# When VectorE makes the low half of a weight split in the attentions, and when it takes the difference of the two maps

## The chip, the cores and the metric

The kernel runs on one core of a Trainium2 chip. The metric is the device time of one execution in microseconds (us), the median of three runs. TensorE (PE) does the matrix products and the transposes, ScalarE (ACT) the activations, VectorE (DVE) the elementwise work and the row reductions, GpSimd (POOL) the small reciprocal square roots, and SyncE (SP) issues the loads of the weights.

## The reference, cut to what matters

Four transformer layers over 256 tokens of width 1024, batch 1, float32. The first two (`first_block`) have a sparse attention and a gated unit; the next two (`second_block`) are these:

```python
def second_block(x, c, ...):
    cond = silu(c)
    for layer in range(2):
        sh1, sc1, g1, sh2, sc2, g2 = split(cond @ ada_w[layer] + ada_b[layer], 6)
        h = modulate(rms_norm(x, norm_mix[layer]), sh1, sc1)
        y = even_mixer(h, ...) if layer % 2 == 0 else odd_mixer(h, ...)
        x = x + g1 * y
        h = modulate(rms_norm(x, norm_mlp[layer]), sh2, sc2)
        x = x + g2 * squared_relu_mlp(h, mlp_w1[layer], mlp_w2[layer])
```

The even mixer has a latent attention with 8 heads (called the MLA attention below) and a dilated attention. The odd mixer has a differential attention and a block attention (MoBA). In the differential attention each head has two maps, and their difference meets the values:

```python
sc = einsum('bqhmd,bkhmd->bmhqk', q, k) * scale      # m: two maps
p = softmax(where(causal, sc, NEG_INF))
pd = p[:, 0] - lam * p[:, 1]
o = einsum('bhqk,bkhe->bqhe', pd, v)
```

## The kernel before, in words

**Products.** Every product is made of three single-pass products: weights and activations are split into a high half and a low half (high x high, high x low, low x high, lines 1422 to 1424). The activations are stationary (XTH/XTL or HTH/HTL, 128 x 128), the weights move, 512 (or 384) columns at a time, and the sum stays in a PSUM bank. The 256 tokens are two tiles t = 0, 1.

**Weight split.** The weights come as items of up to 4 x 512 columns. SP loads an item into a buffer of `RAW` (9 buffers, which share their memory with `WB`). `split` then has two parts: ScalarE copies the raw item into another buffer as the high half (printed L1545, the line of ScalarE's helper), and VectorE subtracts it from the raw item, in place, which gives the low half (L1745). VectorE's part waits for ScalarE's (`wh`), and TensorE's product waits for VectorE's (`wl`). Up to three items are split ahead of their use.

**Order.** Nothing schedules at run time. The program first writes one list, `order`, with calls `do(part, ...)`; then each engine's program walks through the list and emits its own instructions of each part. So each engine does its work strictly in the order of the list. `advance()` puts the splits of the next items into the list, ahead of the products (`slot`) of the current one.

**Attention.** `attention(units, ...)` works on units (some heads of one tile of 128 queries), in steps k. In a step it lists:

1. `scores(k)`: TensorE's products into PSUM, and `soft(k)`: VectorE's row maximum (L1938) and its negative (L1948), then ScalarE's exponentials with row sums into `E`;
2. `turns(k-1)`: TensorE's transposes of the unit before (L1447), after two or three filling products (`busy`, L1407), and a copy of them into `PET`, by ScalarE or VectorE (L1818) in turn;
3. the filler: some steps of a generator with other work, here the products of later input projections, with their splits, their copies to `H`, and the norm and rotation of queries and keys. One such rotation (`qk_rope`, called a rotation below) is five operations of VectorE: L2086, L1861, L1862, L1864, L1865. A sum of squares (`qk_sq`, L2081) follows ScalarE's square, and POOL's reciprocal root comes between the two;
4. `ends(k)` for a unit with `diff`: `differ`, VectorE's difference of the two maps in `E` (L1957, L1960, L1964 twice, L1968 twice), for which the transposes of the next step wait; and `ends(k-1)` for a unit with `joint` (one small sum, L1952);
5. `values(k-2)`: TensorE's products with the values (L1532).

The three attentions with units that concern this case are the MLA attention (6 units), the dilated one (8 units, `joint`) and the differential one (4 units, `diff`). Units 0 and 1 of the differential attention have 128 keys, units 2 and 3 have 256. Its filler makes two input projections (4 items), four rotations and, after step 3, the transposes of the rotated queries and keys of MoBA (`turn_qk`, L1447 <- H). When a tile's values are complete, `diff_out` copies them to `MIX`, squares them into `SCR` (ScalarE) and sums them up (VectorE, L2113); a rotation uses `SCR` too, and the square waits for the rotation listed before it.

## Time and profile before

| | |
|---|---|
| Median of 3 runs | 1432.17 us (1431.86 to 1433.95) |
| The profiled execution's own time | 1432.39 us |
| Its span, first to last instruction | 1430.6 us |
| PE busy | 1343.2 us (94%) |
| DVE busy | 942.3 us (66%) |
| ACT busy | 657.7 us (46%) |
| POOL busy | 109.4 us (8%) |
| Mean granted TensorE clock | 0.984 of full speed |

All times in the text are us from the start of the span. Busy times are shares of that one execution. "Idle before <- releaser" behind an instruction is how long its engine stood still before it, and which instruction let it go on. A start is exact, while the duration of an instruction overlaps the next one's on ScalarE and VectorE, so the distance from start to start is what counts in a sum.

### The profile page before, as it was taken

How to read it: one execution, taken by the hardware profiler on the slowest of the kernel's cores; microseconds unless marked ns; L12 is line 12 of the kernel's file. 1: busy time of each engine (PE TensorE's matmuls, PEld its weight loads, DVE VectorE, ACT ScalarE, POOL GpSimd, SP SyncE). 2: the span in 40 equal slices, each digit the busy share in tenths (PEclk: the TensorE clock that was granted, in tenths of full speed). 3: DMA queues.
4: the chain of work that ended last, by engine and by line, in shares of the span. 5: the costliest groups of instructions: out<-in, count | busy, mean ns of one | idle time of the engine just before them, and what ended most of it. 6: DMA issues, size and time to landing. Idle time of an engine off the chain costs nothing.

```text
span 1430.6 us, 16545 instructions
## 1 busy us (share of the span) xinstructions
PE 1343.2 (94%) x6684; PEld 1108.5 (77%) x6684; DVE 942.3 (66%) x1249; ACT 657.7 (46%) x886; POOL 109.4 (8%) x156
## 2 busy tenths in 40 slices
PE   6999999999989999999798898999998978999998
PEld 6767888887967788888698876888886857788886
DVE  4857777766675777775657856766666776554444
ACT  4544533333463543333365454454545544454542
POOL 1010000000020000000114300000003320000000
PEclk9999999999999999999998999999999999999999
DMA  9505577773612667775153204666663430355550
GB/s 366 194 1 206 219 307 295 293 270 124 272 60 93 229 246 294 294 294 200 61 195 107 100 30 148 264 263 266 262 267 139 156 118 1 118 206 186 188 186 30
DMA packets 40236, 269.87 MB, mean 189 GB/s; under 512 B 4544, under 2 KB 4560, under 8 KB 11872
## 3 DMA queue, kind: packets, MB, share of 16 engines
q1 hardware_dynamic: 37712, 259.31, 48.6%
q0 software_dynamic: 2304, 8.46, 1.6%
q8 instruction: 53, 0.87, 0.2%
q10 hardware_dynamic: 144, 1.05, 0.2%
q14 instruction: 23, 0.19, 0.0%
HBM read 267.75 MB, written 1.05 MB: 188 GB/s over the span
## 4 chain that ended last, share of the span: by engine, by line
PE 81%; DVE 10%; ACT 4%; issue 2%; POOL 1%; DMA 1%; SPq 0%; POOLq 0%; ACTq 0%; DVEq 0%
PE ps L1422 23%; PE ps L1424 23%; PE ps L1423 23%; PE ps L1447 5%; PE ps L1532 2%; PE ps L1508 1%; ACT WB L1545 1%; DVE WB L1745 1%; PE ps L1435 1%; PE ps L1407 1%; DMA RAW<-W 1%; DVE st L2008 1%; DVE X L2018 1%; ACT E L1545 1%; DVE st L1938 1%
## 5 line engine op out<-in xcount | busy, mean ns | idle before, releaser
L1745 DVE TENSOR_TENSOR WB<-RAW,WB 128x2048 fp32r<-128x2048 f32 (+4 forms) x210 | 453.3, 2162 | 285.0 <-ACT WB L1545 284.9
L1545 ACT ACTIVATE WB<-RAW 128x2048 fp32r<-128x2048 f32 (+4 forms) x210 | 379.7, 1810 | 233.0 <-PE ps L1424 220.2
L1422 PE MATMUL ps<-WB,XTH 128*128 128x512 f32 (+3 forms) x1176 | 459.6, 391 | 19.9 <-DVE XTL L1750 12.9
L1424 PE MATMUL ps<-WB,XTL 128*128 128x512 f32 (+3 forms) x1176 | 449.5, 382 | 0.0
L1423 PE MATMUL ps<-WB,XTH 128*128 128x512 f32 (+3 forms) x1176 | 449.1, 382 | 0.0
L1422 PEld LDWEIGHTS ps<-WB,XTH 128*128 128x128 f32 x1176 | 224.4, 191 | 60.8 <-DVE XTL L1750 13.2
L1424 PEld LDWEIGHTS ps<-WB,XTL 128*128 128x128 f32 x1176 | 224.0, 190 | 38.6
L1423 PEld LDWEIGHTS ps<-WB,XTH 128*128 128x128 f32 x1176 | 224.7, 191 | 35.0
L1422 PE MATMUL ps<-WB,HTH 128*128 128x512 f32 (+1 forms) x452 | 178.5, 395 | 2.5 <-DVE HTL L1826 1.9
L1424 PE MATMUL ps<-WB,HTL 128*128 128x512 f32 (+1 forms) x452 | 177.8, 393 | 0.0
L1423 PE MATMUL ps<-WB,HTH 128*128 128x512 f32 (+1 forms) x452 | 177.7, 393 | 0.0
L1804 DVE SCALAR_TENSOR_TENSOR ACC<-RAW,colv,ACC 128x512 f32<-128x512 f32 x168 | 126.2, 751 | 5.1
L1545 ACT ACTIVATE HTH<-ps 128x512 fp32r<-128x512 f32 (+1 forms) x58 | 32.1, 585 | 159.6 <-PE ps L1447 159.4
L1422 PEld LDWEIGHTS ps<-WB,HTH 128*128 128x128 f32 x452 | 85.2, 188 | 22.1 <-DVE HTL L1826 2.4
L1344 POOL TENSOR_SCALAR st<-st 128x1 f32<-128x1 f32 (+3 forms) x42 | 24.3, 578 | 1004.6 <-DVE st L2011 538.3
L1424 PEld LDWEIGHTS ps<-WB,HTL 128*128 128x128 f32 x452 | 85.2, 188 | 19.5
L1423 PEld LDWEIGHTS ps<-WB,HTH 128*128 128x128 f32 x452 | 85.3, 189 | 19.1
L1545 ACT ACTIVATE GB<-ps 128x512 f32<-128x512 f32 (+1 forms) x94 | 46.4, 499 | 93.4 <-PE ps L1424 93.3
L1545 ACT ACTIVATE E<-ps,st 128x128 f32<-128x128 f32 (+1 forms) x104 | 42.4, 420 | 74.5 <-DVE st L1948 74.5
L1826 DVE TENSOR_TENSOR HTL<-ps,HTH 128x512 fp32r<-128x512 f32 x54 | 35.8, 687 | 39.9 <-ACT HTH L1545 39.9
L1407 PE MATMUL ps<-cstb 128*128 128x512 bf16 x228 | 61.6, 386 | 0.0
L1346 POOL TENSOR_TENSOR st<-st,cst 128x1 f32<-128x1 f32 (+3 forms) x42 | 46.5, 1107 | 3.5
(177 smaller groups left out, 1045.0 us busy)
## 6 DMA issues: line engine op xcount, KB each, us to landing
RAW<-W SPq DMA_DIRECT2D x220, 1024.0 KB, 4.9
RAW<-W SPq DMA_DIRECT2D x14, 768.0 KB, 4.3
RAW<-W SPq DMA_DIRECT2D x12, 728.0 KB, 5.7
VEC<-vecd POOLq DMA_DIRECT2D x10, 512.0 KB, 7.1
RAW<-W SPq DMA_DIRECT2D x8, 512.0 KB, 3.3
RAW<-W SPq DMA_DIRECT2D x4, 576.0 KB, 3.8
GB<-xTd ACTq DMA_DIRECT2D x1, 1024.0 KB, 7.9
X<-xd SPq DMA_DIRECT2D x1, 1024.0 KB, 15.9
```

The costliest lines, as they stand in the source:

```text
L1344: eng.tensor_scalar(x, x, scale, eps, ALU.mult, ALU.add).then_inc(*own.up())
L1346: eng.tensor_tensor(x, x, MH.to_broadcast([128, x.shape[1]]), ALU.pow).then_inc(*up("rsqrt", key))
L1407: eng.matmul(banks[b][:, :], identb, cstb[:, 0:512], start=True, stop=True)
L1422: eng.matmul(ps, xh, hi[:, j, c0:c0 + cw], start=first and j == 0, stop=False)
L1423: eng.matmul(ps, xh, lo[:, j, c0:c0 + cw], start=False, stop=False)
L1424: op = eng.matmul(ps, xl, hi[:, j, c0:c0 + cw], start=False, stop=last and j == n - 1)
L1447: op = eng.transpose(banks[b][0:rows, j * 128:j * 128 + 128], src, ident)
L1532: op = eng.matmul(banks[b][:, c0:c0 + dv], PET[:, u["i"], blk * 128:blk * 128 + 128], val, start=(j == 0), stop=(j == len(lst) - 1))
L1545: return eng.activation(dst, src, f, **k)
L1745: eng.tensor_tensor(WB[:, it["raw"], 0:w], RAW[:, it["raw"], 0:w], WB[:, it["high"], 0:w].bitcast(F32), ALU.subtract).then_inc(*up("wl", n))
L1804: op = eng.scalar_tensor_tensor(out=ACC[:, a, :], in0=view[:, j, :], scalar=cond[:, kt:kt + 1], in1=ACC[:, a, :], op0=ALU.mult, op1=ALU.add)
L1826: eng.tensor_tensor(HTL[:, r2:r2 + 2, :], banks[b][:, :].rearrange("p (n q) -> p n q", n=2), HTH[:, r2:r2 + 2, :].bitcast(F32), ALU.subtra ...
```

## The change

`split` becomes two parts with names of their own: `high` (ScalarE) and `low` (VectorE). Outside of attentions both stand side by side in the list as before. Inside `attention` (`cur["lag"]`) the item goes on a list `low`, and its low half is listed later: at the next `advance()`, ahead of its own product, or right behind the `scores`/`soft` of the next step, whichever comes first. And `ends` of a unit with `diff` stands ahead of the filler, directly behind `turns`. `mid_at` is a new argument that nothing sets.

```diff
+        def lows(its=None):
+            for it in list(low) if its is None else [it for it in its if it in low]:
+                low.remove(it)
+                do("low", it)
+
         def advance(most=NBUF):
             loads()
+            lows()
...
-                    do("split", it, after)
+                    do("high", it, after)
+                    low.append(it)
+                    if not cur["lag"]:
+                        lows()
...
             def slot(it, t):
                 b, fr = ps[t]
+                lows([it])
...
+            cur["lag"] = True
             for k in range(n + 2):
                 if k < n:
                     if "bank" not in units[k]["ok"]:
                         units[k]["ok"]["bank"] = take()
                     scores(units[k], 0 if k else first)
+                lows()
                 if 1 <= k <= n:
                     turns(units[k - 1], pads[k - 1] if k <= len(pads) else 2)
+                if k < n and units[k]["diff"]:
+                    ends(units[k])
                 if filler is not None:
                     for _ in range(steps if isinstance(steps, int) else steps[k]):
                         next(filler, None)
-                if k < n and units[k]["diff"]:
-                    ends(units[k])
                 if 1 <= k <= n and units[k - 1]["joint"]:
                     ends(units[k - 1])
                 if k >= 2:
                     values(units[k - 2])
+            cur["lag"] = False
+            lows()
```

No instruction is added or taken away, and TensorE, ScalarE, POOL and SP keep their order, instruction by instruction. Only VectorE's order moves, at three places. The changed kernel's line numbers are 19 higher here (L1745 becomes L1764, L2081 becomes L2100, L1938 becomes L1957).

**Place 1, VectorE, MLA attention, around the row maximum of unit 3** (the fourth low half, 128x1536). Before:

```order
L2081 TENSOR_REDUCE st<-TB 128x6
L1745 TENSOR_TENSOR WB<-RAW,WB 128x1536
L1938 TENSOR_REDUCE st<-ps 128x2
L1948 TENSOR_SCALAR st<-st 128x2
L2086 TENSOR_TENSOR H<-H,st 128x384
L1861 TENSOR_TENSOR SCR<-H,TB 128x384
```

Changed:

```order
L2100 TENSOR_REDUCE st<-TB 128x6
L1957 TENSOR_REDUCE st<-ps 128x2
L1967 TENSOR_SCALAR st<-st 128x2
L1764 TENSOR_TENSOR WB<-RAW,WB 128x1536
L2105 TENSOR_TENSOR H<-H,st 128x384
L1880 TENSOR_TENSOR SCR<-H,TB 128x384
```

The low half went from ahead of the row maximum to behind it. The same holds for the second and third low half (units 1 and 2); the first stands behind two sums of squares and not ahead of them. In the dilated attention one low half and one small sum changed places.

**Place 2, VectorE, differential attention, unit 2** (with its row maximum, its difference, and the rotation of the filler). Before:

```order
L1948 TENSOR_SCALAR st<-st 128x4
L1745 TENSOR_TENSOR WB<-RAW,WB 128x2048
L2086 TENSOR_TENSOR H<-H,st 128x512
L1861 TENSOR_TENSOR SCR<-H,TB 128x512
L1862 TENSOR_TENSOR SCR<-H,TB 128x512
L1864 TENSOR_TENSOR H<-SCR 128x8x32
L1865 TENSOR_TENSOR H<-SCR 128x8x32
L2081 TENSOR_REDUCE st<-GB 128x8
L1957 RECIPROCAL st<-st 128x4
L1960 TENSOR_SCALAR st<-st,lam 128x2
L1964 TENSOR_SCALAR E<-E,st 128x256 x2
L1968 SCALAR_TENSOR_TENSOR E<-E,st 128x256 x2
```

Changed:

```order
L1967 TENSOR_SCALAR st<-st 128x4
L1976 RECIPROCAL st<-st 128x4
L1979 TENSOR_SCALAR st<-st,lam 128x2
L1983 TENSOR_SCALAR E<-E,st 128x256 x2
L1987 SCALAR_TENSOR_TENSOR E<-E,st 128x256 x2
L2105 TENSOR_TENSOR H<-H,st 128x512
L1880 TENSOR_TENSOR SCR<-H,TB 128x512
L1881 TENSOR_TENSOR SCR<-H,TB 128x512
L1883 TENSOR_TENSOR H<-SCR 128x8x32
L1884 TENSOR_TENSOR H<-SCR 128x8x32
L2100 TENSOR_REDUCE st<-GB 128x8
```

The difference of unit 2 went ahead of the rotation and the sum, and the low half went behind the row maximum of unit 3, so it stands between that and the difference of unit 3. Units 0, 1 and 3 move alike; the low half of step 1 stands between unit 1's row maximum and the copy to `PET` that precedes its difference.

**Place 3, VectorE, differential attention, step 4** (the copy of unit 3's transposes and the last rotation). Before:

```order
L2113 TENSOR_REDUCE st<-SCR 128x4
L1818 COPY PET<-ps 128x512
L2086 TENSOR_TENSOR H<-H,st 128x512
L1861 TENSOR_TENSOR SCR<-H,TB 128x512
L1862 TENSOR_TENSOR SCR<-H,TB 128x512
```

Changed:

```order
L2132 TENSOR_REDUCE st<-SCR 128x4
L1764 TENSOR_TENSOR WB<-RAW,WB 128x2048
L1837 COPY PET<-ps 128x512
L2105 TENSOR_TENSOR H<-H,st 128x512
L1880 TENSOR_TENSOR SCR<-H,TB 128x512
L1881 TENSOR_TENSOR SCR<-H,TB 128x512
```

The fourth low half of this attention, which stood behind the row maximum of unit 3, now stands ahead of the copy and the last rotation.

## Rows read from the trace of the kernel before

**Rows 1.** The page's part 4: the chain that ended last, by engine

```profile
PE 81%; DVE 10%; ACT 4%; issue 2%; POOL 1%; DMA 1%; SPq 0%; POOLq 0%; ACTq 0%; DVEq 0%
```

**Rows 2.** Waits of PE, 1137 to 1190: total us, times, longest

```profile
PE ps L1447 <- DVE E L1968: 12.0, 3, 5.4
```

**Rows 3.** Timeline of PE, differential attention: start, us, instruction [idle before <- releaser]

```profile
1156.00 0.44 PE L1447 MATMUL ps<-cst,E 128*128 128x128 f32 x2 [3.63 <-DVE E L1968]
...
1169.00 0.66 PE L1447 MATMUL ps<-cst,E 128*128 128x128 f32 x4 [3.01 <-DVE E L1968]
...
1181.63 1.11 PE L1447 MATMUL ps<-cst,E 128*128 128x128 f32 x4 [5.40 <-DVE E L1968]
...
1185.95 1.88 PE L1447 MATMUL ps<-cst,H 128*128 128x128 f32 x8
1187.65 1.07 PE L1532 MATMUL ps<-H,PET 128*128 128x128 f32 x8
```

**Rows 4.** Timeline of DVE, same stretch

```profile
1150.70 0.42 DVE L1818 COPY PET<-ps 128x256 f32<-128x256 f32 x1
...
1155.86 1.28 DVE L1938 TENSOR_REDUCE st<-ps 128x2 f32<-128x512 f32 x2
...
1161.42 2.29 DVE L1745 TENSOR_TENSOR WB<-RAW,WB 128x2048 fp32r<-128x2048 f32 x1 [4.07 <-ACT WB L1545]
1163.62 0.68 DVE L2086 TENSOR_TENSOR H<-H,st 128x512 f32<-128x512 f32 x1
...
1166.95 0.17 DVE L1957 RECIPROCAL st<-st 128x4 f32<-128x4 f32 x1
...
1168.86 1.28 DVE L1938 TENSOR_REDUCE st<-ps 128x2 f32<-128x512 f32 x2
...
1176.84 0.68 DVE L2086 TENSOR_TENSOR H<-H,st 128x512 f32<-128x512 f32 x1
...
1179.57 0.17 DVE L1957 RECIPROCAL st<-st 128x4 f32<-128x4 f32 x1
...
1181.49 0.68 DVE L2113 TENSOR_REDUCE st<-SCR 128x4 f32<-128x512 f32 x1
1182.78 0.69 DVE L1818 COPY PET<-ps 128x512 f32<-128x512 f32 x1 [0.61 <-PE ps L1447]
1183.39 0.68 DVE L2086 TENSOR_TENSOR H<-H,st 128x512 f32<-128x512 f32 x1
```

**Rows 5.** Timeline of ACT, same stretch

```profile
1157.38 0.47 ACT L1545 ACTIVATE E<-ps,st 128x256 f32<-128x256 f32 x1 [4.54 <-DVE st L1948]
...
1159.19 0.39 ACT L1545 ACTIVATE PET<-ps 128x256 f32<-128x256 f32 x1
...
1179.75 0.63 ACT L1545 ACTIVATE SCR<-MIX 128x512 f32<-128x512 f32 x1 [3.49 <-DVE H L1865]
...
1188.76 0.60 ACT L1545 ACTIVATE MIX<-ps 128x512 f32<-128x512 f32 x1 [0.29 <-PE ps L1532]
```

**Rows 6.** Timeline of DVE, MLA attention

```profile
794.92 0.69 DVE L1938 TENSOR_REDUCE st<-ps 128x2 f32<-128x512 f32 x1
...
799.17 1.76 DVE L1745 TENSOR_TENSOR WB<-RAW,WB 128x1536 fp32r<-128x1536 f32 x1 [0.71 <-ACT WB L1545]
801.84 0.69 DVE L1938 TENSOR_REDUCE st<-ps 128x2 f32<-128x512 f32 x1 [0.91 <-PE ps L1514]
...
808.78 0.68 DVE L1938 TENSOR_REDUCE st<-ps 128x2 f32<-128x512 f32 x1
```

**Rows 7.** Timeline of PE, MLA attention

```profile
810.77 0.66 PE L1447 MATMUL ps<-cst,E 128*128 128x128 f32 x4 [3.06 <-ACT E L1545]
```

**Rows 8.** Stretches: us, busy (count) of PE, PEld, DVE, ACT, POOL; granted clock, DMA share, GB/s

```profile
802.60:816.40 13.80, 10.74 (x60) 9.63 (x59) 13.42 (x33) 4.18 (x14) 6.31 (x8) 0.88 0.01 4
...
812.00:815.70 3.70, 3.70 (x14) 3.70 (x13) 3.63 (x10) 0.00 (x0) 2.12 (x3) 0.54 0.00 0
...
1181.60:1187.80 6.20, 6.17 (x30) 6.17 (x31) 4.60 (x8) 1.19 (x2) 1.20 (x2) 0.51 0.00 0
```

More of the change, by code:

```diff
@@ L290, in program @@
         cur = {"chunk": 0, "item": 0, "load": 0, "ahead": 0, "pairs": 3, "acc": 0, "sum": 0, "id": 0, "col": 0, "turn": 0, "buf": 0,
-               "ada": None}
+               "ada": None, "lag": False}
         bufs = [(n, []) for n in range(NBUF)]
+        low = []
         acc_free = [[], []]
@@ L417, in linear, with linear2 @@
             yield
-        def linear2(name, lhs, after, evacs, mid, pad=(0, 0)):
+        def linear2(name, lhs, after, evacs, mid, pad=(0, 0), mid_at=0):
             ia, ib = chunk_items(name), chunk_items(name)
@@ L428, in slot @@
                 its = (ia, ib)[c]
+                lows([it])
                 do("mm", it, t, lhs, [(b, 0, it["w"], (gs[c], t) if it is its[-1] else None)], it is its[0],
@@ L441, in linear2 @@
                             advance(1)
-                    elif it is ia[0]:
+                    elif it is ia[mid_at]:
                         mid()
@@ L471, in one @@
                 end = last and n == len(its) - 1
+                lows([it])
                 do("mm", it, t, lhs, [(ps[t][c][0], c * 512, 512, (g, t, c) if end else None) for c in range(2)],
@@ L1547, in scalar_program, with high @@
             eng.dma_start(GBT, xTd.rearrange("p (k n) -> p k n", k=8)).then_inc(*landed("xT", 0))
-            def split(it, after):
+            def high(it, after):
                 n, w = it["id"], it["n"] * it["w"]
@@ L1728, in diff_out @@
                 act(SCR[:, 0:512], MIX[:, t, 0:512], ACT.Square).then_inc(*up("diff_sq", t))
-            parts = dict(split=split, x0=x0, setup=setup, turn=turn, halves=halves, ffn_turn=ffn_turn,
+            parts = dict(high=high, x0=x0, setup=setup, turn=turn, halves=halves, ffn_turn=ffn_turn,
                          modulate=modulate, hin=hin, lat=lat, gelu=gelu, sel_score=sel_score, sgu_ln=sgu_ln,
@@ L1740, in vector_program, with low @@
             own = Own(events, "dve_own")
-            def split(it, _):
+            def low(it):
                 n, w = it["id"], it["n"] * it["w"]
@@ L2123, in diff_norm @@
                                   ).then_inc(*up("diff_norm", t))
-            parts = dict(split=split, x0=x0, setup=setup, ada=ada, sum=total, turn=turn, halves=halves,
+            parts = dict(low=low, x0=x0, setup=setup, ada=ada, sum=total, turn=turn, halves=halves,
                          ffn_turn=ffn_turn, mod_scale=mod_scale, modulate=modulate, rope_in=rope_in,
```

## The prediction

> **What bounds the kernel now.** I read the chain that ended last first: 81% of it is TensorE, 10% VectorE, 4% ScalarE [rows 1]. So a change of VectorE's order can only pay, or cost, where TensorE stands still for it. The order of the instructions says where to look: nothing moves but VectorE's, in the MLA attention, in the differential one, and by one small swap in the dilated one.
>
> The waits of TensorE in the differential attention have one entry that matters: the transposes wait three times for VectorE's difference, 12.0 us in all [rows 2]. The timeline of TensorE shows them apart: 3.63, 3.01 and 5.40 us [rows 3]. The timeline of VectorE shows why [rows 4]. A low half that stands behind the row maximum waits 4.07 us for ScalarE's high half, because ScalarE does the exponentials first, and the rotation and the difference queue behind it. In the MLA attention TensorE has one such stop, 3.06 us ahead of unit 4's transposes, for ScalarE's exponentials [rows 7], which follow unit 4's row maximum at 808.78 [rows 6]. From 802.6 to 816.4 VectorE is busy for 13.42 of 13.80 us [rows 8]: there it is the bound, without a gap.
>
> **The differential attention.** Durations are taken from start to start, which is what an in-order engine can repeat [rows 4]:
>
> - low half, 128x2048: 1161.42 to 1163.62, 2.20 us;
> - rotation and one sum of squares: 1163.62 to 1166.95, 3.33 us; rotation alone: 1176.84 to 1179.57, 2.73 us;
> - difference of a unit with 256 keys: 1166.95 to 1168.86, 1.91 us;
> - copy to `PET`: 1182.78 to 1183.39, 0.61 us;
> - from a row maximum at 1155.86 to ScalarE's first exponential at 1157.38, 1.52 us, and 1.81 us from there to the copy behind the last one [rows 4, 5]. The next instruction of VectorE can start about 1.4 us after the maximum.
>
> Now the new list, from the copy at 1150.70, until which TensorE has waited for nothing. One low half goes in ahead of it and nothing goes out before unit 2's maximum, so that maximum starts at 1155.86 + 2.20 = 1158.06. (Unit 1's difference still comes earlier: the 3.3 us of rotation and sum go behind it, against 2.20 us of low half. This shortens the first stop from 3.63 to about 2.5 us.) The exponentials of unit 2 end at 1158.06 + 1.52 + 1.81 = 1161.4. The difference follows directly: 1163.3. TensorE wants unit 2's transposes about then, so the second stop goes. Rotation and sum: 1166.6. Unit 3's maximum starts there, 2.2 us earlier than 1168.86. Then 1.4 for it and 2.20 for the low half: 1170.2 (the exponentials end at 1166.6 + 3.3 = 1169.9), and the difference ends at 1172.1. TensorE takes unit 3's transposes at 1172.2 and not at 1181.63.
>
> That is 9.4 us earlier, but it is not what is won, because **the last rotation is late next**. TensorE's following block, the eight transposes of the rotated keys that started at 1185.95 [rows 3], needs it. VectorE: rotation 2.73 (1174.8), ScalarE's square, which waits for that rotation's use of `SCR` and takes 0.63 [rows 5] (1175.5), its sum 0.68 (1176.2), the low half that now stands ahead of the copy 2.20 (1178.4), the copy 0.61 (1179.0), and the rotation until TensorE's release, 1185.95 - 1183.39 = 2.56. The sum is 1181.6, against 1185.95: **4.3 us won**. TensorE stands still ahead of it: its blocks from 1181.63 to 1185.95 took 4.32 us at half rate and about 2.2 us at full rate, so they are done by 1174.4, and an idle of 7.2 us follows.
>
> **What the clock takes back.** From 1181.6 to 1187.8 the granted clock was 0.51 of full speed [rows 8], that is 1.2 of 2.4 GHz, behind an idle of 5.40 us. The transposes at 1185.95 ran in it already; unit 3's values at 1187.65 took 1.07 us until the copy to `MIX` at 1188.76 [rows 3, 5], which is nearly full rate. After 7.2 us of idle I expect the same clock behind it, and for longer: the values would take about 1.0 us more, and the scores of MoBA's first unit, on which the next maximum waits, some tenths. I take 1.3 us, between 0 (the clock as before) and 2.1 (values and scores both at half rate). Won in this attention: 3.0 us, between 2.2 and 5.1 (the last if the transposes, too, ran at the full rate, 0.85 less).
>
> The Trainium skill, "TensorE: Matmul & The Clock Gate", section "HAM oscillation — how this bites in real kernels", says that idle gaps beyond a certain length send the clock to half, each one anew. The trace bears it out for the stops of 3.63 and 5.40 us but not for the 3.01 us one, behind which the clock stayed full. By the rule one long gap costs one slow stretch, as the single one of 5.40 us did, and the 3.0 us stand.
>
> **The MLA attention.** Four low halves of 128x1536 move, 1.76 us each [rows 6]. Count them between the row maxima. Between those of units 1 and 2 the third goes out and the second comes in; between 2 and 3 the fourth goes out and the third comes in: the same work, so the maxima at 794.92 and 801.84 stay [rows 6]. Between those of units 3 and 4 nothing goes out and the fourth comes in, where VectorE has no gap [rows 8]. The 0.71 us and 0.91 us that VectorE waited around the fourth low half [rows 6] can't pay for it, since the maximum at 801.84 waits for TensorE's scores. Unit 4's maximum goes from 808.78 to 810.5, and TensorE's stop from 3.06 to 4.8 us: **1.7 us lost**. Bounds: nothing, if some gap absorbs it, and 3.4 if the longer stop also brings a second slow stretch like that from 812.0 to 815.7, where a clock of 0.54 over 3.70 us [rows 8] cost about 1.7.
>
> **The rest, at nothing.** In the dilated attention the low half waits for ScalarE, and the small sum slips in ahead of it. The products need each low half late: the first one that moves in the differential attention is used by the block behind 1156.00, the last two by the output projection behind 1188.76. No DMA, buffer or bank changes its order.
>
> **Sum.** -3.0 + 1.7 = -1.3 us. On the profiled execution's 1432.39 us this is 1431.1, on the median, 0.2 us lower, 1430.9.
>
> **The rivals.**
>
> 1. *The forecast*: a small gain in one attention, most of it paid in the other; -1.3 us. Chance 0.50.
> 2. *Only the gain.* The MLA low half is absorbed or mostly so (by POOL or ScalarE setting the pace there and not VectorE), and the clock comes back early: -4.3 us, 1427.9. For it: the clock behind a stop isn't tied to its length alone [rows 3, 8]. Against it: 13.42 of 13.80 us busy. Chance 0.20.
> 3. *All three stops go*: -12.0 us and +1.7, 1421.9. That needs the last rotation in time, 7 us before VectorE can have it. Chance 0.03.
> 4. *No effect*: the clock takes back all that VectorE gives; within 0.5 us of 1432.2. Chance 0.17.
> 5. *Slower, by the clock.* The merged idle of 7.2 us leaves TensorE at half rate well into MoBA, where it is on the chain: one more stretch like that from 1181.6 to 1187.8, 6.20 us at 0.51 [rows 8], costs 3.0 us, on top of the upper bound of 2.1 above. With the second slow stretch in the MLA attention: -4.3 + 2.1 + 3.0 + 3.4 = +4.2, 1436.4. It decides if the rate is still half at unit 2 of MoBA. For it: the rate stayed half for 6.2 us behind 5.40 us of idle. Against it: by 1187.8 it was back, with no denser work than is there now. Chance 0.10. By the same page of the Trainium skill such stretches come again with each gap, which is this case.
>
> **How the numbers follow.** A measurement of this kernel tells about 0.2%, 2.9 us, from no change. Faster by more: rival 3, most of 2, and a slice of the forecast's lower edge: 0.25. Slower by more: most of 5, 0.09. Within: 0.66. The forecast's own range is 1429.3 to 1432.7 (3.0 and 1.7 with half of their bounds). The range for 8 in 10 takes in rival 4 and most of rival 2: 1427.9 to 1433.6, where the upper end is the worst of both terms, -2.2 + 3.4 = +1.2, with some tenths for the spread of runs.
>
> **What would show it.** In the changed kernel's profile: the wait of TensorE's transposes for `E` in the differential attention falls from 12.0 us to 3 to 5 us; a new stop of 6 to 8 us stands ahead of the eight transposes from `H`, released by the last rotation; the low halves there wait for ScalarE hardly at all; the stop at unit 4 of the MLA attention grows from 3.06 to 4.8 us. The forecast is wrong if that stop doesn't grow, if the rotation's end isn't the release, or if the clock is half well beyond the MoBA scores.

## The result, and the profile after

| | before | changed |
|---|---|---|
| Median, 11 runs each | 1433.04 us (1430.98 to 1434.43) | 1429.39 us (1427.68 to 1430.98) |
| The profiled execution | 1432.39 us | 1430.49 us |
| Its span | 1430.6 us | 1428.7 us |

The ratio of the two is 0.9978, between 0.997 and 0.9985: 3.2 us faster, between 2.1 and 4.3 (the medians themselves lie 3.65 us apart). That is just past the 0.2% that the prediction set as the bound of "no change", and the interval holds the bound. The forecast was 1.3 us faster.

The changed kernel's page, head and parts 1 and 4 (before: [rows 1] for the chain):

```profile
span 1428.7 us, 16545 instructions
...
PE 1342.2 (94%) x6684; PEld 1105.1 (77%) x6684; DVE 941.8 (66%) x1249; ACT 657.2 (46%) x886; POOL 109.8 (8%) x156
...
PE 81%; DVE 11%; ACT 3%; issue 2%; POOL 1%; DMA 1%; SPq 0%; POOLq 0%; ACTq 0%; DVEq 0%
```

The page shows next to nothing: same counts, same shares. The change is in a few stops, and these stand in the waits of PE, stretch 1137 to 1190 of the changed kernel (total us, times, longest):

```profile
PE ps L1466 <- DVE H L1884: 6.7, 2, 6.4
PE ps L1466 <- DVE E L1987: 4.4, 3, 2.5
```

The 12.0 us for the difference [rows 2] became 4.4, and a new wait of 6.7 us for the rotation took most of its place. The timeline of PE, changed kernel, shows them one by one (line numbers here are 19 higher: L1466 are transposes, L1551 values, L1527 scores, L1426 filling products):

```profile
1155.85 0.44 PE L1466 MATMUL ps<-cst,E 128*128 128x128 f32 x2 [2.51 <-DVE E L1987]
...
1164.58 0.66 PE L1466 MATMUL ps<-cst,E 128*128 128x128 f32 x4 [0.33 <-DVE E L1987]
...
1173.41 0.66 PE L1466 MATMUL ps<-cst,E 128*128 128x128 f32 x4 [1.60 <-DVE E L1987]
...
1176.13 0.66 PE L1466 MATMUL ps<-cst,H 128*128 128x128 f32 x4 [0.30 <-DVE H L1884]
...
1183.18 1.09 PE L1466 MATMUL ps<-cst,H 128*128 128x128 f32 x4 [6.40 <-DVE H L1884]
1184.06 1.91 PE L1551 MATMUL ps<-H,PET 128*128 128x128 f32 x8
```

The stops of 3.63, 3.01 and 5.40 us [rows 3] are now 2.51, 0.33 and 1.60, and one of 6.40 us stands ahead of the last four transposes of rotated keys. The timeline of DVE, changed kernel, says what each waits for:

```profile
1159.04 1.28 DVE L1957 TENSOR_REDUCE st<-ps 128x2 f32<-128x512 f32 x2
...
1162.51 0.18 DVE L1976 RECIPROCAL st<-st 128x4 f32<-128x4 f32 x1 [2.00 <-ACT E L1564]
...
1167.76 1.28 DVE L1957 TENSOR_REDUCE st<-ps 128x2 f32<-128x512 f32 x2
1169.07 0.17 DVE L1967 TENSOR_SCALAR st<-st 128x4 f32<-128x4 f32 x1
1169.15 2.28 DVE L1764 TENSOR_TENSOR WB<-RAW,WB 128x2048 fp32r<-128x2048 f32 x1
1171.35 0.17 DVE L1976 RECIPROCAL st<-st 128x4 f32<-128x4 f32 x1
...
1176.83 0.69 DVE L2132 TENSOR_REDUCE st<-SCR 128x4 f32<-128x512 f32 x1 [0.76 <-ACT SCR L1564]
1177.43 2.28 DVE L1764 TENSOR_TENSOR WB<-RAW,WB 128x2048 fp32r<-128x2048 f32 x1
1179.63 0.68 DVE L1837 COPY PET<-ps 128x512 f32<-128x512 f32 x1
1180.23 0.68 DVE L2105 TENSOR_TENSOR H<-H,st 128x512 f32<-128x512 f32 x1
...
1182.62 0.42 DVE L1884 TENSOR_TENSOR H<-SCR 128x256 f32<-128x256 f32 x1
...
1188.76 0.76 DVE L1957 TENSOR_REDUCE st<-ps 128x2 f32<-128x256 f32 x2 [0.77 <-PE ps L1533]
```

The low half at 1169.15 fills the time in which ScalarE makes the exponentials; before, the low half waited there 4.07 us [rows 4], because its high half stood behind them. The one at 1177.43 is different: it stands ahead of the copy and the last rotation, and TensorE waits all through it.

In the MLA attention, the timeline of PE, changed kernel:

```profile
813.35 1.11 PE L1466 MATMUL ps<-cst,E 128*128 128x128 f32 x4 [4.73 <-ACT E L1564]
```

3.06 us [rows 7] became 4.73.

**Where the time went, by stretches.** In one execution the time ahead of the MLA attention, where nothing moved, differs by up to 3.8 us between the kernels of this study, so spans don't compare. The distance between fixed points of the program does. The points are the first scores of the MLA, dilated and differential attentions on TensorE, MoBA's first row maximum on VectorE (1188.76 above, 1190.65 in the kernel before), and the end:

| us | MLA to dilated | dilated to differential | differential to MoBA's maximum | to the end | sum |
|---|---|---|---|---|---|
| before | 54.35 | 307.57 | 53.66 | 239.93 | 655.51 |
| changed | 56.09 | 305.96 | 50.80 | 239.93 | 652.78 |
| difference | +1.74 | -1.61 | -2.86 | 0.00 | -2.7 |

The second column holds what was not foreseen: 1.61 us won in a stretch in which the change moves no more than one low half past one small sum. TensorE's timeline of the two kernels shows where. These are the transposes for the first layer's feed-forward norm, second tile; first the kernel before:

```profile
886.51 1.27 PE L1447 MATMUL ps<-cst,MIX 128*128 128x128 f32 x8 [2.33 <-DVE MIX L2026]
```

then the changed one:

```profile
889.06 1.09 PE L1466 MATMUL ps<-cst,MIX 128*128 128x128 f32 x8 [2.33 <-DVE MIX L2045]
```

The stop is the same to a hundredth. What follows isn't. The stretches behind it (us, busy (count) of PE, PEld, DVE, ACT, POOL; granted clock, DMA share, GB/s), before:

```profile
887.50:890.90 3.40, 3.40 (x11) 2.68 (x10) 3.33 (x8) 2.21 (x6) 0.00 (x0) 0.53 0.25 43
```

and changed, with the stretches behind its two long stops:

```profile
813.60:817.00 3.40, 3.40 (x14) 3.40 (x14) 3.33 (x8) 0.52 (x2) 1.35 (x2) 0.57 0.00 0
...
890.10:893.50 3.40, 3.40 (x17) 2.77 (x16) 3.33 (x8) 2.21 (x6) 0.00 (x0) 1.00 0.21 51
...
1183.20:1189.00 5.80, 5.80 (x29) 4.12 (x31) 1.36 (x3) 1.83 (x3) 0.84 (x2) 0.54 0.00 0
```

Behind 886.5 the clock was at half (1.2 GHz), behind 889.1 at full (2.4 GHz): 11 products against 17 in 3.40 us. At half rate 3.4 us hold the work of about 1.7 us at full rate, and that is, within 0.1 us, the 1.61 us given back.

### The profile page after: what moved, and what is told of

It reads as the page before. It is cut to its first block, busy times and chain, and to the rows that moved or that the text cites. A ratio compares the mean times of both kernels' runs of the same rounds, so it can differ in the third digit from the quotient of the medians.

```text
span 1428.7 us, 16545 instructions
## 1 busy us (share of the span) xinstructions
PE 1342.2 (94%) x6684; PEld 1105.1 (77%) x6684; DVE 941.8 (66%) x1249; ACT 657.2 (46%) x886; POOL 109.8 (8%) x156
## 4 chain that ended last, share of the span: by engine, by line
PE 81%; DVE 11%; ACT 3%; issue 2%; POOL 1%; DMA 1%; SPq 0%; POOLq 0%; ACTq 0%; DVEq 0%
PE ps L1441 23%; PE ps L1443 23%; PE ps L1442 23%; PE ps L1466 4%; PE ps L1551 2%; DVE WB L1764 2%; PE ps L1527 1%; PE ps L1454 1%; PE ps L1426 1%; ACT WB L1564 1%; DMA RAW<-W 1%; DVE st L2027 1%; DVE X L2037 1%; DVE st L1957 1%; DVE X L2040 1%
## 5 line engine op out<-in xcount | busy, mean ns | idle before, releaser
L1764 DVE TENSOR_TENSOR WB<-RAW,WB 128x2048 fp32r<-128x2048 f32 (+4 forms) x210 | 453.2, 2161 | 267.4 <-ACT WB L1564 267.3
L1426 PE MATMUL ps<-cstb 128*128 128x512 bf16 x228 | 63.9, 398 | 0.0
```

The source lines that it names most:

```text
L1426: eng.matmul(banks[b][:, :], identb, cstb[:, 0:512], start=True, stop=True)
L1764: eng.tensor_tensor(WB[:, it["raw"], 0:w], RAW[:, it["raw"], 0:w], WB[:, it["high"], 0:w].bitcast(F32), ALU.subtract).then_inc(*up("wl", n))
```

## The experiments

Two questions: which part earns the gain, and does the MLA attention pay (the forecast's theory: it pays 1.7 us net) or is it paid back (the rival: the clock behind the stop at 886.5 depends on where that stop falls). The sum of stretches, as in the table above, stands beside each median. It agrees within 0.6 us, fourth_late and combo (0.9 us) apart, which says that the one execution shown is a typical one. The edits are shown shortened: `...` stands for what is left out, and a remark behind `#` stands for the argument in the call of `attention`.

| run | MLA to dilated | to differential | to MoBA's maximum | to the end | sum against before | time against before, by the ratio |
|---|---|---|---|---|---|---|
| changed | 56.09 | 305.96 | 50.80 | 239.93 | -2.7 | -3.2 |
| mla_lag_only | 56.08 | 306.07 | 53.60 | 239.93 | +0.2 | +0.3 |
| no_lag_mla | 54.37 | 307.48 | 50.83 | 240.01 | -2.8 | -3.3 |
| lag_only | 56.10 | 305.93 | 50.95 | 239.96 | -2.6 | -2.6 |
| early_only | 54.37 | 307.61 | 51.83 | 241.6 | -0.1 | -0.3 |
| shift_only | 55.92 | 306.03 | 53.68 | 239.93 | +0.1 | +0.4 |
| fourth_late | 55.95 | 310.24 | 48.67 | 240.0 | -0.7 | -4.7 |
| second_fourth_late | 56.01 | 305.99 | 47.68 | 239.97 | -5.9 | -5.9 |
| busy_stop | 56.09 | 305.99 | 48.64 | 241.57 | -3.2 | -3.4 |
| norm_pads | 54.38 | 309.40 | 52.82 | 243.5 | +4.6 | +4.3 |
| combo_no_norm | 54.36 | 307.58 | 46.16 | 241.6 | -5.8 | -5.6 |
| combo | 54.40 | 309.41 | 46.18 | 243.4 | -2.1 | -3.0 |
| combo_mid | 54.35 | 307.55 | 46.16 | 239.97 | -7.5 | -8.0 |

### One part alone

**mla_lag_only**: the late low halves in the MLA attention alone.

```diff
-            cur["lag"] = True
+            cur["lag"] = lag          # True for the MLA attention, else False
-                if k < n and units[k]["diff"]:
-                    ends(units[k])
                 if filler is not None:
...
+                if k < n and units[k]["diff"]:
+                    ends(units[k])
```

> Only the MLA attention has its low halves one unit later; the differences stay behind the filler and all other low halves where they were. Theory A (the terms of the prediction are right, the clock's part apart): unit 4's row maximum comes 1.7 us later, TensorE's stop ahead of unit 4's transposes grows from 3.06 to 4.7-4.8 us, and the time is 1.7 us above before (+0.12%). Theory B (the MLA term is paid back on the average, by the clock or by slack behind it): the stop grows the same, the time is within 0.5 us of before.

Measured: 1432.68 us, ratio 1.0002 (0.9994 to 1.0011). The MLA stretch is 1.73 us longer, the next one 1.50 shorter. So the part forecast at 1.7 us lost costs nothing that the total shows: +0.3 us, between -0.9 and +1.6.

**no_lag_mla**: the change without its MLA part.

```diff
-            cur["lag"] = True
+            cur["lag"] = lag          # False for the MLA attention, else True
```

> The change as it is, but for the MLA attention, where each low half stands beside its high half again. Theory A: 1.7 us below the changed kernel, so about 4.9 us below before (-0.34%), the stop in the MLA attention back at 3.06 us. Theory B: as the changed kernel, about 3.2 us below before (-0.22%).

Measured: 1429.32 us, ratio 0.9977 (0.9969 to 0.9986), the changed kernel's time. The other side of the same finding: without the MLA stop of 4.73 us nothing is won, since the half rate behind the norm's stop is back. The stop in the timeline of PE, no_lag_mla:

```profile
885.27 1.19 PE L1466 MATMUL ps<-cst,MIX 128*128 128x128 f32 x8 [2.34 <-DVE MIX L2045]
```

and the stretch behind it:

```profile
886.40:889.80 3.40, 3.40 (x10) 2.71 (x9) 3.33 (x7) 2.21 (x6) 0.00 (x0) 0.54 0.28 48
```

**lag_only**: the low halves late everywhere, the difference back behind the filler.

```diff
-                if k < n and units[k]["diff"]:
-                    ends(units[k])
                 if filler is not None:
...
+                if k < n and units[k]["diff"]:
+                    ends(units[k])
```

> All low halves one unit later, the differences behind the filler as before. From the rows: unit 2's maximum 2.2 us later as in the change, but rotation and difference fill VectorE's wait for the exponentials, so unit 3's maximum is bound by TensorE's scores at 1166 to 1167; the first stop of TensorE grows to 5.8 us, and the last rotation ends at 1180 to 1182 on the clock of before, about where it does in the change (1181.6). Theory A (the lag earns the gain, the early difference little or nothing): -3 to -4.3 us there, +1.7 in the MLA attention, in all as the changed kernel within 1 us. Theory C (the early difference earns the gain): the time is that of before or above, +1.7 us.

Measured: 1429.95 us, ratio 0.9982 (0.9974 to 0.9991). Its waits of PE, same stretch:

```profile
PE ps L1466 <- DVE E L1987: 6.5, 2, 5.8
PE ps L1466 <- DVE H L1884: 3.6, 1, 3.6
```

TensorE waits about as long in all (10.1 us against the change's 11.1), only elsewhere. The last rotation lets it go 46.32 us behind this attention's first scores, against 45.22 in the changed kernel, so the difference's place is worth 1.1 us there. It hardly shows in MoBA's maximum (0.15 us later), because the clock gave it back: behind this shorter stop of 3.56 us it was full for 1.0 us more (0.99 from 1184.3 to 1185.3, then 0.50 up to 1188.7).

**early_only**: the difference early, the low halves as before.

```diff
-            cur["lag"] = True
+            cur["lag"] = False
```

> The differences ahead of the filler, no low half moved. From the rows: low halves three and four still wait for ScalarE (1.5 us and 0.3 us in place of 4.07 and 4.29), and the last rotation ends at 1183.4 on the clock of before, 2.5 us earlier than 1185.95. Theory A: 1 to 2.5 us below before, with no loss in the MLA attention. Theory C (the early difference earns the whole gain): 3.2 us below before or more, as the changed kernel without its MLA loss, -4.9 us.

Measured: 1432.06 us, ratio 0.9998 (0.999 to 1.0007); one of its 12 runs, at 1918.96 us, stands far from all others and doesn't touch the median. The stretch of the differential attention is 1.83 us shorter, but the last one is 1.7 us longer: behind the second layer's stop for its norm, 2.32 us, the clock is at half, where before, behind the same stop of 2.33 us, it was at full. Row of early_only:

```profile
1242.10:1245.50 3.40, 3.40 (x10) 2.67 (x10) 2.02 (x5) 1.58 (x4) 0.00 (x0) 0.56 0.00 0
```

So in the total the late low halves make -2.6 of -3.2 us, and the early difference alone gives -0.3 us, not told from nothing. On the spot both pay, and overlap: 2.71 us for the low halves alone, 1.83 us for the difference alone, 2.86 us for the two. What early_only won there went to the half rate in the last stretch. It was expected at 1 to 2.5 us below before.

### Is it the place of the stop in time?

**shift_only**: the kernel before, its order untouched, with 11 filling products ahead of the dilated attention's first scores.

```diff
-            attention(units, 0.125, fill, first=3 if i else 0)
+            attention(units, 0.125, fill, first=3 if i else 11)
```

> The kernel before, with 11 filling products ahead of the first scores of the dilated attention in place of 3 fewer waits: TensorE's timeline from there on lies about 1.6 us later, as in the kernels with the MLA attention's low halves late, and VectorE's order is that of before. Theory D (what pays the MLA loss back is only that the timeline lies 1.6 to 1.7 us later when TensorE stops for 2.3 us ahead of the transposes for the first layer's feed-forward norm, at 886.5, so that the clock isn't cut behind that stop): the granted clock behind the stop at about 888 is full, as in the three kernels with the lag, and the time is within 0.5 us of before although 1.6 us of work was added. Theory E (the low halves' order itself, or the attention's other transfers, keep the clock up): the clock behind that stop is half as before, and the time is 1.6 us above before.

Measured: 1433.46 us, ratio 1.0003 (0.9994 to 1.0012). The first scores of the dilated attention in the timeline of PE, before and shift_only:

```profile
829.42 0.68 PE L1508 MATMUL ps<-T 64*128 64x128 f32 x6 [0.76 <-DVE T L1818]
...
829.41 2.54 PE L1407 MATMUL ps<-cstb 128*128 128x512 bf16 x11
831.88 0.71 PE L1508 MATMUL ps<-T 64*128 64x128 f32 x6
```

The filling products take 2.47 us from start to start and fill a stop of 0.76 us, so that the MLA to dilated stretch is 1.57 us longer. The time is 0.4 us longer, not told from nothing. The norm's stop in the timeline of PE, shift_only:

```profile
889.03 1.09 PE L1447 MATMUL ps<-cst,MIX 128*128 128x128 f32 x8 [2.34 <-DVE MIX L2026]
```

and the stretch behind it:

```profile
890.00:893.40 3.40, 3.40 (x17) 2.78 (x16) 3.33 (x8) 2.22 (x6) 0.00 (x0) 1.00 0.21 43
```

This settles it. With no low half moved, the same stop of 2.34 us, 1.6 us later than in the kernel before, is followed by the full clock. By the second column of the table, the executions with this stop unchanged fall in two groups: about 306.0 us where the first stretch is 1.6 to 1.7 us longer (changed, mla_lag_only, lag_only, shift_only, second_fourth_late, busy_stop), about 307.5 where it isn't (before, no_lag_mla, early_only, combo_no_norm). In fourth_late, whose first stretch is 1.6 us longer too, full clock follows this stop as well (1.00 from 886.0 to 889.4); its 310.24 us come from other places, below.

What sorts the executions is not the time from the start of the span, which the earlier part of the program shifts. It is the distance from the first scores of the MLA attention to the end of the stop. The norm's stop ended 111.4 to 111.7 us behind them in the six executions with half rate behind it (before, no_lag_mla, early_only, norm_pads, combo_no_norm, combo) and 113.0 to 113.2 us in the seven with full clock. Two of them stand at nearly the same time: a stop that ended at 887.20 in second_fourth_late, and one at 887.31 in combo_no_norm. The stretches behind them, in this order:

```profile
888.00:891.40 3.40, 3.40 (x18) 2.82 (x17) 3.33 (x8) 2.22 (x6) 0.00 (x0) 1.00 0.15 31
...
888.30:891.50 3.20, 3.20 (x9) 2.52 (x9) 3.13 (x8) 2.02 (x6) 0.00 (x0) 0.50 0.18 26
```

### Is the last rotation what is late next?

**fourth_late**: the change, with the fourth low half behind the copy and the rotation again.

```diff
-                lows()
+                if k not in hold:      # hold=(4,) in the differential attention
+                    lows()
```

> The change, with the differential attention's fourth low half behind the last rotation and not ahead of the copy to PET. Theory A (the last rotation is what is late next, and this low half of 2.20 us is on its way): the rotation ends 2.2 us earlier, TensorE's stop ahead of the last transposes shrinks from 6.40 to 4.2 us, and the time is 1.5 to 2.2 us below the changed kernel, 4.7 to 5.4 below before. Theory F (the stop is bound by something else as well, the values or the square): less than 0.5 us below the changed kernel.

Measured: 1428.33 us, ratio 0.9967 (0.9955 to 0.998). The last stop fell from 6.40 to 4.20 us, the length of the low half, and MoBA's maximum came 2.13 us earlier. By the ratios the time is 4.7 us below before, 1.5 us below the change. Its profiled execution is no typical one: it has further stretches at half rate, from 904.2 to 907.5 and from 1088.5 to 1095.3, and the second column is 4.3 us longer than in the changed kernel. That is about what lies between the sum (-0.7) and the time (-4.7).

**second_fourth_late**: the same with the second low half too (`hold=(1, 4)`).

> As fourth_late, and the second low half behind unit 2's row maximum, where VectorE now waits 2.00 us for ScalarE's exponentials, instead of ahead of unit 0's copy to PET. Theory A: unit 2's maximum is back at its place of before, the wait is filled, the last rotation ends about 4 us earlier than in the changed kernel and TensorE's first stop goes; time 3 to 4 us below the changed kernel, 6 to 7 below before. Theory F: no more than fourth_late.

Measured: 1427.46 us, ratio 0.9959 (0.9946 to 0.9971). Waits of PE, same stretch:

```profile
PE ps L1467 <- DVE H L1885: 4.5, 2, 4.2
PE ps L1467 <- DVE E L1988: 3.7, 3, 1.7
```

Here the line numbers are one higher again. The differential stretch is another 0.99 us shorter; the times of the two runs don't tell it (five executions each, overlapping intervals). It is less than foreseen: 3.1 us below the change on the spot and 2.7 by the ratio, for 3 to 4, and the first stop shrank to 1.65 us and did not go. Both low halves fill no gap of VectorE where the change puts them; the one behind unit 3's maximum does.

### What does the clock take back behind the merged stop?

**busy_stop**: the change, with 24 filling products ahead of the last transposes of rotated keys, where TensorE stood still.

```diff
-                    [lambda: turn_qk(4, 0, 12, twm), lambda: turn_qk(4, 1, 12, twm)]])
+                    [lambda: turn_qk(4, 0, 12, twm), lambda: turn_qk(4, 1, 12, twm, 24)]])
```

> The change, with 24 filling products (0.215 us each at full rate, 5.2 us) in TensorE's last stop of 6.40 us, ahead of the last four transposes. Theory A (the idle cuts the clock, which costs 1 to 2 us in transposes, values and MoBA's first scores): the granted clock from 1183 to 1189 is full and not half, MoBA's first row maximum comes 1.5 to 2.3 us earlier, and the time is as much below the changed kernel. Theory G (the rate behind the stop doesn't depend on what TensorE does in it, or doesn't matter to the chain): within 0.5 us of the changed kernel.

Measured: 1429.21 us, ratio 0.9976 (0.9966 to 0.9986). Timeline of PE, busy_stop:

```profile
1177.14 5.34 PE L1426 MATMUL ps<-cstb 128*128 128x512 bf16 x24
1183.61 0.66 PE L1466 MATMUL ps<-cst,H 128*128 128x128 f32 x4 [1.13 <-DVE H L1884]
1184.11 1.06 PE L1551 MATMUL ps<-H,PET 128*128 128x128 f32 x8
```

and the stretch from there:

```profile
1183.60:1187.10 3.50, 3.49 (x31) 2.60 (x33) 1.17 (x3) 1.82 (x3) 0.00 (x0) 1.00 0.00 0
```

The rotation releases TensorE as late as before, but the clock behind it is at full, and MoBA's maximum comes 2.16 us earlier. That is the clock's whole share in this attention. The time didn't fall by it: the last stretch grew by 1.64 us, with half rate behind the second layer's norm stop, as in early_only.

### Putting it together

**combo_no_norm**: no lag in the MLA attention, `hold=(1, 4)`, and 16 filling products in the last stop.

```diff
-            cur["lag"] = True
+            cur["lag"] = lag          # False for the MLA attention
...
-                lows()
+                if k not in hold:      # hold=(1, 4) in the differential attention
+                    lows()
...
-                    [lambda: turn_qk(4, 0, 12, twm), lambda: turn_qk(4, 1, 12, twm)]])
+                    [lambda: turn_qk(4, 0, 12, twm), lambda: turn_qk(4, 1, 12, twm, 16)]])
```

> second_fourth_late with 16 filling products (3.4 us) in its stop of 4.20 us, and the MLA attention's low halves beside their high halves. Theory A (terms add up): -1.7 in the MLA attention against second_fourth_late and -1.0 to -1.9 behind the filled stop; where the clock is cut behind the norm stops, +1.6 each. In all 1.1 to 3.6 us below second_fourth_late, 7.0 to 9.5 below before. Theory B: what is won in the MLA attention is given back at the norm stop, about 7 below before.

Measured: 1426.9 us, ratio 0.9961 (0.9947 to 0.9974). The differential stretch is 7.50 us shorter than before, and both norm stops are followed by half rate (from 888.2 and from 1236.3). In time it is 5.6 us below before, less than the 7 and more that were foreseen, and, within the noise, what second_fourth_late has: what the MLA attention (1.65 us) and the filled stop (1.52 us) gave against it went to half rate behind the two norm stops (1.59 and 1.6 us).

**norm_pads**: the kernel before, with 10 filling products ahead of the feed-forward norm's transposes, meant to keep TensorE busy in the stop of 2.33 us.

```diff
                 if t:
-                    go(0)
+                    go(0, pad=10)
```

> The kernel before, with 10 filling products (2.15 us) in each of the two stops of 2.33 us ahead of the transposes for a feed-forward norm (886.5 and 1242.8 in before's profile). Theory D (the clock is cut behind these stops or not by where they lie in time, at a price of 1.6 us): the clock behind 886.5 is full, nothing else moves, 1.6 us below before in the profile and 0.8 to 1.6 on the average of the runs. Theory E (the stop isn't what cuts it): within 0.5 us of before, with the half rate still there.

Measured: 1436.8 us, ratio 1.003 (1.0018 to 1.0042): slower by 4.3 us. It missed its stop. `go(0)` is the first tile's norm, and the stop belongs to the second's. The timeline of PE, norm_pads, has the stop as before, 2.11 us:

```profile
885.69 1.49 PE L1447 MATMUL ps<-cst,MIX 128*128 128x128 f32 x8 [2.11 <-DVE MIX L2026]
```

Half rate followed it as before, and two more stretches at half rate came, from 1091.0 and from 1244.6, worth about 1.6 and 1.7 us. The filling itself made the way to the norm's stop 0.24 us longer in the first layer and 1.87 us in the second. In the differential stretch 0.83 us came back, and the sum is the 4.6 us of the table.

The half rate from 1091.0 stands behind a stop of 3.5 us, ahead of the transposes for a norm, which every kernel here has. In the kernel before, the full clock follows it. Timeline of PE and the stretch behind, before:

```profile
1090.49 1.09 PE L1447 MATMUL ps<-cst,MIX 128*128 128x128 f32 x8 [3.52 <-DVE MIX L2026]
...
1090.60:1094.00 3.40, 3.40 (x20) 2.93 (x21) 3.40 (x6) 2.14 (x5) 3.40 (x6) 1.00 0.00 0
```

That stop ended 315.4 to 315.6 us behind the MLA attention's first scores in the eleven executions with full clock behind it, and 315.7 us in norm_pads and combo, with half rate behind it. The 0.24 us that the filling added in the first layer are enough to make that difference. Fourth_late has half rate there as well, at 317.1 us.

**combo**: combo_no_norm with the edit of norm_pads (`go(0, pad=10)`).

> combo_no_norm with norm_pads' filling products in both norm stops. Theory A and D: no cut behind either stop, the MLA term is kept: 8 to 9.5 us below before, 1425 to 1423.5. Theory B: as combo_no_norm.

Measured: 1428.95 us, ratio 0.9979 (0.997 to 0.9988), 3.0 us below before and not the 8 to 9.5 that theory A and D foresaw. Half rate still follows both norm stops. Against combo_no_norm the same two things cost again: half rate behind the stop of 3.50 us (from 1092.8), 1.6 us, and the filling in the second layer, 1.8 us.

**combo_mid**: combo_no_norm with the filling products where the second tile's norm waits.

```diff
-            mid = (lambda go=go: go(1, pad=2))
+            mid = (lambda go=go: go(1, pad=12))
```

> combo_no_norm with 12 filling products, not 2, ahead of the transposes of the second tile for each feed-forward norm, which is where the stops of 2.33 us at 886.5 and 1242.8 are (norm_pads and combo had them ahead of the first tile's, another place). Theory D: the stops shrink from 2.33 to about 0.2 us with the engine busy, the granted clock behind both is full, the MLA term of 1.7 us is kept: 1.6 us (one cut on the average of the runs) to 3.2 us (both, as in combo_no_norm's profile) below combo_no_norm, 7.2 to 8.8 below before, 1425 to 1423.4. Theory E (these stops aren't what cuts the clock): within 0.5 us of combo_no_norm.

Measured: 1424.84 us, ratio 0.9944 (0.9931 to 0.9958), 8.0 us below the kernel before and the fastest of all. Timeline of PE at the norm's stop, combo_mid:

```profile
884.41 2.76 PE L1427 MATMUL ps<-cstb 128*128 128x512 bf16 x12
...
887.36 1.09 PE L1467 MATMUL ps<-cst,MIX 128*128 128x128 f32 x8 [0.18 <-DVE MIX L2046]
```

The stop is 0.18 us and no half rate follows it. In this execution half rate (0.50) stands from 905.3 to 908.7 instead, behind a stop of only 1.19 us and eight products of one column, which every kernel has. So the second stretch (307.55) won nothing; what was won over combo_no_norm is in the last one (241.6 to 239.97). The intervals of the two kernels overlap.

## Why the prediction was right, and where it was off

**The differential attention, in order.** Its first scores stand 0.97 us later in the changed trace, which is added to each forecast start:

| step | forecast | measured |
|---|---|---|
| first stop | about 2.5 | 2.51 |
| unit 2's maximum | 1159.03 | 1159.04 |
| second stop | gone | 0.33 |
| unit 3's maximum | 1167.6 | 1167.76 |
| unit 3's transposes | 1173.2 | 1173.41 |
| the copy to `PET` | 1179.4 | 1179.63 |
| TensorE released by the last rotation | 1182.6 | 1183.18 |
| the idle ahead of it | 7.2 | 6.40 |
| TensorE's waits for `E` | 3 to 5 | 4.4 |

The forecast time lay in its range, and this attention came out as forecast. The order was followed with start-to-start durations, and up to the last copy VectorE was never more than 0.4 us behind the forecast. The low halves no longer wait for ScalarE: the waits of VectorE have no entry for it. One size was off: the transposes came 3.74 us earlier and not 4.3. VectorE was 0.25 us late at the copy. The rest, 0.4 us, is a reading of the rows: the 2.56 us from the rotation's start to "TensorE's release" were too short, because at 1185.95 the rotation had not ended. Timeline of DVE, before:

```profile
1185.77 0.41 DVE L1865 TENSOR_TENSOR H<-SCR 128x256 f32<-128x256 f32 x1
```

So the first transposes of that block didn't wait for it. The changed trace shows the same from the other side: four of the eight ran at 1176.13, and only four were left for the last rotation, which gave 0.82 back. The values started 4.56 us earlier.

**The clock's share.** Forecast 1.3 us (values 1.0, scores some tenths). From the values' start to the copy to `MIX` (1184.06 to 1186.02, before 1.11 [rows 3, 5]) it was 0.85, and from there to MoBA's maximum another 0.85: 1.70 us. With that, 4.56 - 1.70 = 2.86 us won, against the forecast 3.0. busy_stop bears the size out: 2.16 us come back when the clock stays full, the four slow transposes included. It stayed inside the bounds of 0 to 2.1 for this term.

**The MLA attention is the step that failed**, and with it "The rest, at nothing". "1.7 us lost" was right on the spot: 1.74 us, the stop 4.73 for a forecast 4.8, no second slow stretch. It was wrong as a term of the sum, because the clock behind the stops outside the two attentions was put at nothing without a look at them. The forecast took a delay that nothing absorbs as lost time, and looked for gaps of VectorE that could absorb it. What gave it back was no gap: the same delay moved a later stop to where the clock stays full behind it, 75 us on. mla_lag_only (+0.3 us in time), no_lag_mla (no difference to the change) and shift_only (the same with no low half moved) show it. The sum should have been -2.9 + 1.7 - 1.6 = -2.8, which lies in the measured -2.1 to -4.3; the forecast -1.3 doesn't. The time of 1429.39 us lies in the range for 8 in 10 (1427.9 to 1433.6) because that was made wide for other rivals, and in the forecast's own (1429.3 to 1432.7) by 0.1 us: so far the hit is luck. That own range doesn't quite come out of its rule either, since half of each bound gives 1429.0 to 1432.1.

**The rivals.** *Only the gain* had the nearest difference (-4.3 us) for the wrong reason: the low half was not absorbed, and in the differential attention the clock came back no earlier. *No effect* and *all three stops go* fall. *Slower, by the clock* falls as well: half rate ended by 1189.0, not in MoBA's second unit. But its thought, that a stop's price lies in the clock behind it, is what decided early_only and busy_stop: each shortened the differential stretch by about 2 us (against before and against the change) and met half rate in the last one. Its rule by length alone doesn't hold: stops of 3.01 and 3.52 us had full clock behind them, one of 2.33 us had not.

**Left open.** How the clock comes to sort the stops by where they fall: the traces show that it does, and no more. And why fourth_late's profiled execution differs from its median. It differs early: the half rate in which the MLA attention's first scores run ends 6.4 to 6.6 us behind their start in the 13 other profiled executions and 5.3 us in this one, so that the clock's changes lie elsewhere against the program. Whether its other four executions were like the 13 no trace shows.

## What to carry to other kernels

Work that an in-order engine must do can go where the engine would wait for another one, and only there: of the low halves in the differential attention, the one behind unit 3's row maximum paid, and the two that stand ahead of a copy, a difference or a rotation cost 1.0 and 2.1 us. Follow the list past the stop that goes, to what is late next.

A sum of differences on the spot isn't the end of it where TensorE stops for 2 us or more elsewhere: a shift of the timeline by 1 or 2 us, in one place by 0.3 us, can switch a stretch at half rate on or off there, worth 1.6 us each. Compare distances between fixed points, look at the granted clock behind every stop, and where a stop can't be removed, give TensorE products to do in it. Look behind the shorter stops too: in combo_mid half rate came behind one of 1.19 us.

## What the runs showed of the hardware

**The same stop, two clocks.** A stop of 2.3 us was followed by 3.4 us at 1.2 GHz (0.53, 0.54, 0.56) or by the full clock (1.00), by where it fell and not by its length. In the first layer half rate followed the one that ended at 886.5 (before) and not the one at 889.1 (changed); in the second it followed the one at 1240.3 (early_only) and not the one at 1242.8 (before). Stops of 3.01 us [rows 3] and 3.52 us were followed by no half rate, one of 2.33 us was. In 13 executions the distance from the MLA attention's first scores sorts the first layer's stop without an exception: 111.4 to 111.7 us half, 113.0 to 113.2 us full. The Trainium skill, "TensorE: Matmul & The Clock Gate", section "What's actually happening", says that the activity is watched in a window that runs freely and isn't reset by the kernel. The traces agree in that the place counts beside the length. No run shows the window itself. That medians follow the one profiled execution within 0.6 us for most kernels says that the place is nearly the same from execution to execution. So does the half rate around the MLA attention's first scores, whose end lies within 0.2 us of the same place in 13 of 14 profiled executions. A window with no tie to the program wouldn't give that by itself; no run here tells why.

**A shift pays or costs nothing.** 11 filling products, which put all that follows 1.57 us later on the path, cost 0.4 us of time with an interval that holds zero.
